# A fused attention/retention layer: how the softmax shift rows are made from the row maxima

## What is computed

```
def gqa_block(q, k, v):
    B, Q = q.shape[:2]
    qg = q.reshape(B, Q, ATTN_KV_HEADS, GQA_GROUP, HEAD_DIM)
    s = jnp.einsum('bqkgd,btkd->bkgqt', qg, k, preferred_element_type=jnp.float32) * ATTN_SCALE
    p = jax.nn.softmax(s, axis=-1).astype(v.dtype)
    o = jnp.einsum('bkgqt,btkd->bqkgd', p, v)
```

## Time and profile before

| | us |
|---|---|
| median of 3 runs | 1481.38 |
| the runs | 1478.02, 1481.70, 1481.38 |
| the profiled execution | 1482.69 |
| its span | 1480.9 |

### The profile page before, as it was taken

The page is one execution under the profiler, slowest core; times in us unless marked ns, Lnnn a source line. Parts: engine busy times, 40 slices in busy tenths (PEclk is TensorE's granted clock), DMA queues, the critical chain, the costliest instruction groups (busy, mean ns, idle before and its releaser), DMA issues.

```text
span 1480.9 us, 16623 instructions
## 1 busy us (share of the span) xinstructions
PE 1413.3 (95%) x6132; PEld 1100.7 (74%) x6132; DVE 914.7 (62%) x1232; ACT 539.6 (36%) x754; POOL 104.9 (7%) x117
## 2 busy tenths in 40 slices
PE   5899999999969999999999999999979999999996
PEld 4688887666738888888885377777858888888885
DVE  5756687785166666663235675889647888886222
ACT  2423254554352322322222454332444333342221
POOL 0001630000300000000110020000010000000010
PEclk9799999999979999999999999999999999999998
DMA  9334431022216666674421022220212223233211
GB/s 369 118 117 125 142 95 35 31 98 86 85 54 245 213 217 222 203 238 174 154 82 43 27 73 72 71 100 29 72 64 93 99 86 103 94 100 127 98 58 57
DMA packets 44514, 169.19 MB, mean 114 GB/s; under 512 B 5516, under 2 KB 6092, under 8 KB 43181
## 3 DMA queue, kind: packets, MB, share of 16 engines
q1 hardware_dynamic: 43052, 165.60, 33.0%
q0 software_dynamic: 1408, 2.89, 0.7%
HBM read 163.49 MB, written 2.10 MB: 112 GB/s over the span
## 4 chain that ended last, share of the span: by engine, by line
PE 90%; DVE 6%; ACT 1%; DMA 1%; issue 1%; SPq 0%; POOL 0%; DVEq 0%; ACTq 0%
PE PS L611 72%; PE PS L981 4%; PE PS L877 2%; PE PS L668 2%; DVE tb L1717 2%; PE PS L1104 1%; DVE H L1717 1%; PE PS L631 1%; DMA wraw<-w_mod_a 1%; PE PS L656 1%; PE PS L842 1%; PE PS L843 1%; PE PS L739 1%; PE PS L865 1%; PE PS L864 1%
## 5 line engine op out<-in xcount | busy, mean ns | idle before, releaser
L611 PE MATMUL PS<-H,wsp 128*128 128x512 f32 x3600 | 840.2, 394 | 21.5 <-DVE H L1717 18.0
L611 PEld LDWEIGHTS PS<-H,wsp 128*128 128x128 f32 x3600 | 678.6, 189 | 176.6 <-issue 22.0
L600 DVE TENSOR_TENSOR wsp<-wraw,wsp 128x1024 fp32r<-128x1024 f32 (+1 forms) x182 | 237.7, 1306 | 414.4 <-ACT wsp L594 413.9
L594 ACT ACTIVATE wsp<-wraw 128x1024 fp32r<-128x1024 f32 (+1 forms) x182 | 202.7, 1114 | 522.8 <-PE PS L611 521.8
L611 PE MATMUL PS<-hid,wsp 128*128 128x512 f32 x1056 | 240.0, 389 | 0.0
L611 PEld LDWEIGHTS PS<-hid,wsp 128*128 128x128 f32 x1056 | 198.1, 188 | 41.9 <-issue 0.8
L1717 DVE SCALAR_TENSOR_TENSOR cva<-PS,dert,cva 128x441 f32<-128x441 f32 (+2 forms) x176 | 122.3, 695 | 5.5
L1901 DVE CUSTOM_DVE_ANT_0 sink<-mring,crow_t,colt 128x1024 bf16<-128x1024 f32 x56 | 71.7, 1280 | 0.8 <-DMA mring<-mod_c 0.4
L1640 POOL COPY acc<-sqb 128x512 f32<-128x512 f32 x4 | 4.4, 1096 | 788.9 <-ACT sqb L1432 288.1
L1643 POOL TENSOR_TENSOR acc<-acc,sqb 128x512 f32<-128x512 f32 x24 | 41.2, 1718 | 202.0 <-ACT sqb L1618 82.6
L668 PE MATMUL PS<-sqb,ones 128*128 128x512 f32 (+1 forms) x64 | 35.1, 702 | 8.9 <-ACT sqb L1145 8.9
(11 more groups left out here) (278 smaller groups left out, 1298.2 us busy)
## 6 DMA issues: line engine op xcount, KB each, us to landing
mring<-mod_c SPq DMA_DIRECT2D x56, 512.0 KB, 4.7
wraw<-w_ffn_in SPq DMA_DIRECT2D x44, 512.0 KB, 3.3
wraw<-w_up SPq DMA_DIRECT2D x44, 512.0 KB, 3.2
wraw<-w_hy_in SPq DMA_DIRECT2D x24, 512.0 KB, 3.2
wraw<-w_w_in SPq DMA_DIRECT2D x22, 512.0 KB, 3.3
wraw<-w_ffn_out SPq DMA_DIRECT2D x16, 704.0 KB, 4.2
wraw<-w_down SPq DMA_DIRECT2D x16, 704.0 KB, 4.1
mfirst<-mod_x SPq DMA_DIRECT2D x12, 512.0 KB, 16.9
```

Of the source, the lines that this page charges most:

```text
L594: nc.scalar.activation(wsp[:, o % 2, 0, 0:n], wraw[:, g % RAW, 0:n], ACT.Copy).then_inc(w_hi, 1)
L600: nc.vector.tensor_tensor(wsp[:, o % 2, 1, 0:n], wraw[:, g % RAW, 0:n], wsp[:, o % 2, 0, 0:n].bitcast(F32), ALU.subtract).then_inc(w_lo, 1)
L611: mm = nc.tensor.matmul(psum, wsp[:, o % 2, a, wk * P:(wk + 1) * P], h[:, b, kt, :], start=first and kt == kts[0] and (a, b) == (0, 0), st ...
```

## The change

The two parts of the shift are now made before the product. `att_diagonal` first writes the negated maxima of the head, 128x4, rounded to fp32r (`nmx[:, 0]`), then what the rounding left (`nmx[:, 1]`), and then two 128x512 diagonals of type fp32r, `Dg[0]` and `Dg[1]`, one for each part. `shift_row` issues two fp32r products that accumulate into bank 4. Their weights are windows of 128 columns of a new tile `pick` that is zero but for one column of ones: the first window has that column at the partition of the high part, the second 32 further. Bank 4 so holds the high part in one partition, the low part in the other, and zeros elsewhere. ScalarE's copy (`shift_high`) stays; `shift_low` and its semaphore `a_ml` are gone, and `scores(h, 0)` waits for `a_mh`, ScalarE's copy. `pick` is written once, in DVE's loop over the input projection at n = 19. `Dg[1]` lies on tiles that the retention has finished with.

```diff
@@
-        Dg = sb("Dg", o_r + 16 * K + LA // P * VW * 4, [P, 4, P])
+        Dg = [sb("Dg0", o_r + 16 * K + LA // P * VW * 4, [P, 4, P], F32R), sb("Dg1", o_r + 12 * K, [P, 4, P], F32R)]
+        pick = sb("pick", o_r + 87 * K, [P, 96 + P], F32R)
@@
+        nmx = sb("nmx", o_r + 87 * K + 896, [P, 2, 4], F32R)
@@ shift_row, scores
-                nc.tensor.matmul(PS[:, 4, :], ones[:, :], Dg[:, :, :].rearrange("p a b -> p (a b)"), start=True,
-                                 stop=True).then_inc(a_row, 1)
+                for v in range(2):
+                    at = 96 - ((1 - h % 2) * HD + 32 * v)
+                    mm = nc.tensor.matmul(PS[:, 4, :], pick[:, at:at + P], Dg[v][:, :, :].rearrange("p a b -> p (a b)"),
+                                          start=v == 0, stop=v == 1)
+                mm.then_inc(a_row, 1)
...
-                    pe.wait_ge(a_ml, h + 1)
+                    pe.wait_ge(a_mh, h + 1)
@@ DVE, the loop of the input projection
+                if n == 19:
+                    dve.wait_ge(r_u, 1)
+                    VE.tensor_scalar(pick[:, 0:P], ident[:, :], 0.0, None, ALU.mult)
+                    own(VE.tensor_scalar(pick[:, P:P + 96], ident[:, 0:96], 0.0, None, ALU.mult))
+                    own(VE.tensor_scalar(pick[:, 96:97], ident[:, 0:1], 0.0, 1.0, ALU.mult, ALU.add))
@@ att_diagonal
-                stt(Dg[:, :, :], ident[:, :].unsqueeze(1).to_broadcast([P, 4, P]), -float(D),
-                    der("mx", 4 * h, 4).unsqueeze(2).to_broadcast([P, 4, P]), ALU.mult, ALU.mult).then_inc(a_dg, 1)
-
-            def shift_low(h):
-
-                t, e = h // 2, h % 2
-                first = (1 - e) * HD + 32
-                rows = slice(first, first + 32)
-                dve.wait_ge(a_mh, h + 1)
-                VE.tensor_tensor(q_low(t, e)[rows, :], PS[rows, 4, :], q_low(t, e)[rows, :].bitcast(F32),
-                                 ALU.subtract).then_inc(a_ml, 1)
+                own(VE.tensor_scalar(nmx[:, 0, :], der("mx", 4 * h, 4), -1.0, None, ALU.mult))
+                own(stt(nmx[:, 1, :], der("mx", 4 * h, 4), -1.0, nmx[:, 0, :].bitcast(F32), ALU.mult, ALU.subtract))
+                for v in range(2):
+                    ins = VE.tensor_tensor(Dg[v][:, :, :], ident[:, :].unsqueeze(1).to_broadcast([P, 4, P]),
+                                           nmx[:, v, :].bitcast(F32).unsqueeze(2).to_broadcast([P, 4, P]), ALU.mult)
+                ins.then_inc(a_dg, 1)
@@ the calls
-            shift_low(0)
...
-                if h < 7:
-                    shift_low(h + 1)
```

More of the change, by code:

```diff
@@ L302, in build @@
         a_kh, a_kl, a_qh, a_ql = sem("a_kh"), sem("a_kl"), sem("a_qh"), sem("a_ql")
-        a_s, a_mx, a_dg, a_row, a_mh, a_ml = (sem("a_s"), sem("a_mx"), sem("a_dg"), sem("a_row"), sem("a_mh"),
-                                              sem("a_ml"))
+        a_s, a_mx, a_dg, a_row, a_mh = sem("a_s"), sem("a_mx"), sem("a_dg"), sem("a_row"), sem("a_mh")
         a_st, a_exp, a_pv, a_r, a_o, a_h, a_lo = (sem("a_st"), sem("a_exp"), sem("a_pv"), sem("a_r"), sem("a_o"),
```

## The result

| | before | with the change |
|---|---|---|
| median of 11 runs, us | 1478.02 | 1483.3 |
| lowest to highest | 1474.11 to 1481.7 | 1479.34 to 1486.47 |
| span of the profiled execution | 1480.9 | 1483.7 |
| granted clock over the span | 0.98 | 0.981 |

The ratio is 1.0033 (95% interval 1.0021 to 1.0046): 4.9 us slower, from 3.1 to 6.8. The 11 runs of the kernel before include the three shown ahead of the prediction, and their median is 3.4 us lower; the forecast's 1485.2 is best read as its +3.8. That lies inside the interval, and the result lies 0.5 us beyond the 4.4 us that I had called the edge; the interval reaches to both sides of it.

What follows compares the result with a forecast made beforehand. A circle of PE and DVE, both nearly full, was taken to bound the kernel. Later diagonals 8.08, less cheaper products 2.92, less slack 1.40, gave +3.8 us: 1485.2 us, range 1480.5 to 1489.5.

Steps and rivals of the forecast that it cites:

- the edge: About 0.3%, 4.4 us: what a measurement of this kernel can tell from no change; the forecast lay close to it.
- diagonals later, 8 heads: DVE, last maximum to last diagonal's end: 1.73 us instead of 0.72, so 1.01 later per head, 8.08 in all.
- product cheaper, waiting heads: PE's shift row, heads where PE waited before: the fp32r pair saves 0.39 us each, for six heads.
- product cheaper, heads 6 and 7: PE's shift row, heads where PE had not waited before: the fp32r pair saves 0.29 us each.
- slack lost, heads 6 and 7: Diagonals there were early, with 0.70 us to spare each; 1.40 us is taken off the added time.
- shift_low: Removing this 0.68 us DVE instruction per head, and the scores' wait for it, is worth nothing.
- pick: Its three one-time DVE instructions at n = 19, about 0.3 + 0.2 + 0.15 us, cost zero.
- loop: Attention over eight heads, DVE's last maximum of head 0 to PE's first output-projection product: +3.8 us.
- the narrow steps cost more: Rival: DVE's 128x4 instructions cost more than 0.205 us each; +8.0 us at the upper bound of 0.47; chance 0.20.
- the pair isn't cheap: Rival: PE's two fp32r products cost what the fp32 product did; +6.7 us; chance 0.05.
- PE was the bound all along: Rival: DVE makes up the longer diagonals from its idleness, only the savings remain; -2.9 us; chance 0.08.
- The clock falls: Rival: PE idles ahead of shift rows and one period runs at 1.2 GHz; +15 us; chance 0.02.

Runs made afterwards that it cites:

- third diagonal: Changed kernel with one more 128x512 diagonal, which nobody reads, written between the two: loop 106.68 us; when run again, 106.73 us and ratio 1.0077 to the kernel before.
- the high part alone: Changed kernel with one fp32r diagonal and one fp32r product, the low part of the shift left out: loop 90.84 us, ratio 0.9968 to the kernel before.
- the wait for each diagonal: Changed kernel with each of the two products waiting only for its own diagonal: loop 96.92 us, ratio 1.0016 to the kernel before.
- the moved row: Changed kernel with DVE's modulation row of iterations 1 to 4 moved from between the maxima to behind the diagonal: loop 95.71 us, ratio 1.0008.
- The third product: Changed kernel with one more fp32r product per shift row, adding the low diagonal twice: loop 100.64 us, one run of 1483.23 us.
- Filling PE's pauses: Changed kernel with 4 and 7 overwritten products ahead of the shift rows of heads 0 and 1: loop 99.16 us, ratio 1.0033 to the kernel before.

## Why the prediction was right

| term | forecast, us | measured |
|---|---|---|
| diagonals later, 8 heads | 8 x 1.01 | 1.73 after the last maximum, so 8 x 1.01; a third diagonal added 0.59 to 0.62 a head |
| product cheaper, waiting heads | 6 x 0.39 | 0.96 to 0.56 |
| product cheaper, heads 6 and 7 | 2 x 0.29 | 0.86 to 0.57 |
| slack lost, heads 6 and 7 | 2 x 0.70 | periods 11.55 and 11.57 for 11.6 |
| shift_low | 0 | loop 95.27 for 95.26 without it |
| pick | 0 | ends 1.97 us before what DVE waits for |
| loop | +3.8 | +3.53, again +3.58 |

The chosen 0.205 for the narrow steps was 0.20. The table's 58 cycles plus one a column, by which the Trainium skill (VectorE: DVE Perf Modes, TRN2 errata) would have given an estimate of 0.065 us, stayed off by about the same factor as in the earlier trace rows: the records say 0.17 and 0.16. The sum by that table, put at below 1.4 us, is 8 x 0.72 - 4.32 = 1.44; nothing hangs on it.

What the sum missed is small, 0.23 us, and 0.14 of it lie at head 0: 12.77 instead of 12.29 + 1.01 - 0.39 = 12.91. Before, the matmul behind shift_row(0) started 1.00 us behind it and the next but one 0.53 later; now these are 0.57 and 0.45. Before, that matmul (266.12) started 0.15 us behind the end of an ACT copy (265.97), much as with the high part alone, where the profile names this wait; with the change the copy is done 0.71 us ahead of it. That the sum had left this wait out is read from the timelines, not tried by itself.

Of the rivals, "the narrow steps cost more" and "the pair isn't cheap" fall with the table. "PE was the bound all along" falls with the third diagonal, which came out at full price on DVE, with the wait for each diagonal and with the moved row, in both of which PE has the same work and the loop is shorter. The third product says nothing on it: it would have cost its full price on a bound PE too. "The clock falls" did not happen in the traces of the changed kernel, as forecast, but it was nearer than the 0.02 I gave it: 0.6 us more of waiting brought it at two heads. Its price was too high, though: I had put 11 us on a period, and the two falls cost 2.21 - 0.6 = 1.6 and 2.03 - 0.6 = 1.4 us.

The chances fit what came: 0.59 for no change, 0.38 for slower, and the measured 0.33% stands just beyond the line of 0.3% between them, with an interval on both sides. Which side of it a measurement falls on is luck; the mechanism and the 3.5 us of the loop are not. What stays open is the 1.1 to 1.4 us between the loop's 3.5 and the ratios' 4.7 and 4.9. Every ratio of the study holds its loop's difference inside its interval, but those with two diagonals lie above it each time (2.4 us for 1.7, 4.7 for 3.6, 4.9 for 3.9, 1.2 for 0.5). Those with three diagonals do not (8.1 us for 8.8, 11.4 for 11.5), nor do those with one, which have `pick` as well (-4.7 for -4.4, -5.9 for -5.5). So `pick` is hardly the reason, and it may be scatter, since ratios of one chip share their runs of the kernel before. Filling PE's pauses did not remove it, and behind the loop the traces are no longer than before.

## What to carry to other kernels

When two engines wait for each other in a circle, list what stands between the last input and the hand-over: only this counts, an instruction removed from elsewhere on the same engine is worth nothing (nothing here for 8 x 0.68 us of work), and moving a bystander behind the hand-over can be worth more than a faster product (3.1 us against 2.9; with the high part alone it was worth only 1.1, since PE's own work was nearly the bound there). Ask what accuracy a term needs before it is split: a softmax's shift cancels, and leaving its low part out turned +3.5 us into -4.4. Making a waiting TensorE wait longer can cost its clock, so look at the granted clock behind every pause; its length alone does not tell.

## What I had not expected of the hardware

With one more diagonal of 0.60 us, PE's idleness of 1.87 and 2.79 us took the granted clock to 0.57 and 0.79 of two stretches and cost 3.1 us beyond the waiting, in both executions that were profiled; 1.27 and 2.19 us at the same places, in four profiled executions, cost nothing, though 2.19 is more than the 1.87 that did. Useless matmuls in the pauses gave 2.6 us back.
